# Modulation sums and convolution taps as multiply-add chains in PSUM; first three panels k-block by k-block

## The reference, cut to what matters

```python
def adaln(c, w_mod, b_mod):
    mod = jax.nn.silu(c) @ w_mod + b_mod
    return jnp.split(mod, 6, axis=-1)

def modulate(x, g, shift, scale):
    return rmsnorm(x, g) * (1.0 + scale[:, None, :]) + shift[:, None, :]
```

## Time and profile before

| | us |
|---|---|
| median of 3 runs | 2796.45 |
| the profiled execution | 2796.17 |
| its span | 2794.4 |
| PE busy | 2526.6 (90%) |
| DVE busy | 1561.7 (56%) |
| POOL busy | 954.9 (34%) |
| ACT busy | 908.9 (33%) |

### The profile page before, as it was taken

One profiled execution on the slowest core, in us unless ns is written; L12 is line 12 of the kernel. 1 busy time (PEld: TensorE's weight loads), 2 busy tenths in 40 slices (PEclk: granted clock), 3 DMA queues, 4 the chain that ended last, 5 costly groups with the idle time before them and its releaser, 6 DMA issues.

```text
span 2794.4 us, 35608 instructions
## 1 busy us (share of the span) xinstructions
PE 2526.6 (90%) x12106; PEld 2075.1 (74%) x12106; DVE 1561.7 (56%) x2371; ACT 908.9 (33%) x1433; POOL 954.9 (34%) x399
## 2 busy tenths in 40 slices
PE   5687998999998989899999834999999999999998
PEld 4567776787886667788887733888887887888886
DVE  6994567686634785311115995555455745463545
ACT  2150443322233253322224222332225544342222
POOL 1230003444453301344444531444444420344443
PEclk9895799999999899999999966999999999999999
DMA  6532003555432101232322200232223310232322
GB/s 265 173 128 83 1 17 131 178 185 176 147 106 76 61 9 68 75 98 90 99 97 91 83 30 17 96 105 90 98 90 105 98 61 1 83 105 91 98 95 70
DMA packets 71623, 263.70 MB, mean 94 GB/s; under 512 B 7904, under 2 KB 8416, under 8 KB 70880
## 3 DMA queue, kind: packets, MB, share of 16 engines
q1 hardware_dynamic: 68352, 251.01, 27.1%
q10 hardware_dynamic: 3168, 11.34, 1.1%
HBM read 260.22 MB, written 2.10 MB: 94 GB/s over the span
## 4 chain that ended last, share of the span: by engine, by line
PE 71%; issue 14%; DVE 10%; DVEq 2%; POOL 2%; ACT 1%; DMA 0%; POOLq 0%; ACTq 0%; SPq 0%
PE bank L562 21%; PE bank L563 21%; PE bank L564 21%; DVE cout L1808 3%; PE bank L707 2%; POOL w_lo L533 2%; PE bank L695 1%; PE bank L685 1%; DVE acc L1240 1%; DVEq L1801 1%; PE bank L849 1%; DVE tn L1292 1%; DVE h_lo L1287 1%; PE bank L641 1%; DVE modsum L1513 1%
## 5 line engine op out<-in xcount | busy, mean ns | idle before, releaser
L533 POOL TENSOR_TENSOR w_lo<-raw,w_hi 128x1024 fp32r<-128x1024 f32 x378 | 927.7, 2460 | 1811.8 <-ACT w_hi L921 1811.0
L562 PE MATMUL bank<-h_hi,w_hi 128*128 128x512 f32 x1760 | 708.7, 403 | 44.4 <-DVE h_lo L1287 19.5
L563 PE MATMUL bank<-h_lo,w_hi 128*128 128x512 f32 x1760 | 696.1, 396 | 0.0
L564 PE MATMUL bank<-h_hi,w_lo 128*128 128x512 f32 x1760 | 694.7, 395 | 0.0
L921 ACT ACTIVATE w_hi<-raw 128x1024 fp32r<-128x1024 f32 x378 | 393.5, 1052 | 594.9 <-PE bank L564 565.3
L562 PEld LDWEIGHTS bank<-h_hi,w_hi 128*128 128x128 f32 x1760 | 336.7, 191 | 133.6 <-issue 28.4
L562 PE MATMUL bank<-g_hi,w_hi 128*128 128x512 f32 x1072 | 421.5, 393 | 7.2 <-DVE g_lo L1391 5.6
L563 PE MATMUL bank<-g_lo,w_hi 128*128 128x512 f32 x1072 | 419.0, 391 | 0.0
L564 PE MATMUL bank<-g_hi,w_lo 128*128 128x512 f32 x1072 | 418.6, 390 | 0.0
L564 PEld LDWEIGHTS bank<-h_hi,w_lo 128*128 128x128 f32 x1760 | 336.6, 191 | 72.0
L563 PEld LDWEIGHTS bank<-h_lo,w_hi 128*128 128x128 f32 x1760 | 337.1, 192 | 67.6 <-issue 1.2
(11 more groups left out here) (260 smaller groups left out, 2807.6 us busy)
## 6 DMA issues: line engine op xcount, KB each, us to landing
raw<-in_panels SPq DMA_DIRECT2D x378, 512.0 KB, 3.7
modraw<-in_mods SPq DMA_DIRECT2D x80, 512.0 KB, 3.8
first_mods<-in_mods SPq DMA_DIRECT2D x4, 2048.0 KB, 19.8
w<-in_w ACTq DMA_DIRECT2D x2, 2048.0 KB, 8.6
x<-in_x SPq DMA_DIRECT2D x1, 2048.0 KB, 8.2
out<-yout ACTq DMA_DIRECT2D x8, 256.0 KB, 2.2
mask<-in_causal ACTq DMA_DIRECT2D x1, 1024.0 KB, 4.7
mask<-in_dilated ACTq DMA_DIRECT2D x1, 1024.0 KB, 4.8
```

The costliest lines, as they stand in the source:

```text
L533: pool.tensor_tensor(w_lo[:, slot, :], raw[:, slot, :], w_hi[:, slot, :].bitcast(F32), ALU.subtract)\
L562: pe.matmul(out, w_h, m_h, start=start, stop=False)
L563: pe.matmul(out, w_h, m_l, start=False, stop=False)
L564: return pe.matmul(out, w_l, m_h, start=False, stop=stop)
```

## The change

Five things. The sum of a modulation panel over k-blocks becomes a chain of eight instructions, one tensor_scalar and seven scalar_tensor_tensor, whose partial sum stands in PSUM (`CHAIN`, bank 6), with a drain between any two; it takes two panels at once (128x256 elements), which come in one load of 1 MB into one buffer, and PE sums both. The pairs go beside the odd panels up to 73, and beside P_OUT0 + 2, + 4 and + 6. The first 16 columns become four batches, each with two blocks of shift and two of scale; in a batch DVE sums three and PE does one, and the h of two k-blocks follows each batch. The sum of squares of the first norm is added up by PE over eight separate tiles (`sq0`). The first three panels behind the norms of layer 0, of layer 0's FFN, of layer 1 and of layer 1's FFN run k-block by k-block: nine matmuls per block, in three banks (`by_k`). The taps of the first three chunks of the 31-tap convolution are summed in banks 7, 4 and 6, and the last tap writes `cout`; the mixing matmuls move to banks 0 and 1.

```diff
+PAIR_AT = {}
+for _p in range(MOD_UNTIL):
+    if _p % 2 or _p in (P_OUT0 + 2, P_OUT0 + 4, P_OUT0 + 6):
+        PAIR_AT[_p] = len(PAIR_AT)
...
+            def load_pair(m, after):
+                sp_.wait_ge(mod_summed, after)
+                sp_.dma_start(modraw[:, :, :], A["pairs"][m]).then_inc(mod_landed, 16)
...
+            load_first(0)
+            for p in range(3):
                 load_raw(p)
...
+            for n in range(1, BATCHES):
+                load_first(n)
+            load_raw(3)
...
+            for p in range(P_FFN0):
                 load_raw(p + RING, after=p + 1)
...
+                if PAIR_AT.get(p, 0) > 0:
+                    load_pair(PAIR_AT[p], summed(PAIR_AT[p] - 1))
...
+            def first_batch(n):
+                pe.wait_ge(first_landed[n], 16)
+                if n == 3:
+                    pe.wait_ge(first_added, 1)
                 for k in range(KB):
-                    m = pe.matmul(mod_column(q), first_mods[q // 4][:, q % 4, P * k:P * k + P], csil[:, k:k + 1],
-                                  start=(k == 0), stop=(k == KB - 1))
+                    pe.matmul(FIRST_BANK[n][:, 0:1], first_mods[n][:, 0, P * k:P * k + P], csil[:, k:k + 1],
+                              start=(k == 0), stop=(k == KB - 1))
+                pe.wait_ge(mod_summed, n + 1)
+                for w in range(1, 4):
+                    m = pe.matmul(FIRST_BANK[n][:, w:w + 1], modsum[:, w, :], ones[:, 0:1], start=True, stop=True)
                 m.then_inc(mod_used, 1)
-            def mod_panel(slot, summed, out):
-                pe.wait_ge(mod_summed, summed)
-                pe.matmul(out, modsum[:, slot, :], ones[:, 0:1], start=True, stop=True).then_inc(mod_used, 1)
+            def mod_pair(m, summed_value, column):
+                pe.wait_ge(mod_summed, summed_value)
+                for w in range(2):
+                    last = pe.matmul(column(w), modsum[:, 2 * (m % 2) + w, :], ones[:, 0:1], start=True, stop=True)
+                last.then_inc(mod_used, 1)
...
+            def by_k(p, m_hi, m_lo, ready, ks):
+                for k in ks:
+                    pe.wait_ge(h_lo_ready, ready + k + 1)
+                    for slot in range(p % RING, p % RING + 3):
+                        if k == 0:
+                            pe.wait_ge(lo_ready, p + slot - p % RING + 1)
+                            if p >= RING:
+                                pe.wait_ge(bank_free, p + slot - p % RING - RING + 1)
+                        at = slot % RING
+                        wh, wl = w_hi[:, at, P * k:P * k + P], w_lo[:, at, P * k:P * k + P]
+                        m = three(bank[at][:, :], wh, wl, m_hi[:, k, :], m_lo[:, k, :], k == 0, k == KB - 1)
+                        if k == KB - 1:
+                            m.then_inc(panel_done, 1)
...
+                    elif n == 0:
+                        by_k(p, *up, KB * H_OF[r], range(KB))
+                        panel(p + 3, (p + 3) % RING, *up)
+                        for q in range(p, p + 4):
+                            with_mods(q)
+                        begun = 4
+                    panels(p + begun, 2 * size - begun, *up, mods=p < MOD_UNTIL)
...
-            rstd(0)
-            for q in range(MOD_FIRST):
-                if q in ALONE:
-                    first_mod_alone(q)
-                else:
-                    mod_panel(summed(q) % SUMS, summed(q), mod_column(q))
+            for k in range(KB):
+                pe.wait_ge(squares_ready, k + 1)
+                for j in range(QB):
+                    m = pe.matmul(bank[j][:, 0:1], sq0[:, k, P * j:P * j + P], ones[:, 0:1], start=(k == 0), stop=(k == KB - 1))
+            m.then_inc(sums_ready, 1)
+            first_batch(0)
+            spread(0, bank[5], QB)
+            first_batch(1)
+            by_k(0, h_hi, h_lo, 0, (0, 1))
+            first_batch(2)
+            by_k(0, h_hi, h_lo, 0, (2, 3))
+            first_batch(3)
+            by_k(0, h_hi, h_lo, 0, (4, 5, 6, 7))
...
             for n in range(KB):
-                square(0, n, x[:, n, :])
-            take_root(0)
...
+                act.activation(sq0[:, n, :], x[:, n, :], ACT.Square).then_inc(squares_ready, 1)
+            for p in range(3):
+                split_hi(p)
+            act.wait_ge(sums_ready, 1)
+            for j in range(QB):
+                m = act.activation(root[:, j:j + 1], bank[j][:, 0:1], ACT.Sqrt, bias=EPS, scale=1.0 / D)
+            m.then_inc(root_ready, 1)
+            act.dma_start(lruw[:, :, :, :], A["lruw"]).then_inc(lru_landed, 16)
...
-                                sum_mod_loop(it, pg + AHEAD)
-                                sum_mod_loop(it, pu + AHEAD)
+                                m = PAIR_AT[pu + AHEAD]
+                                sum_pair(m, it * 32 + 16 * (m + 1), it * 2 + (summed(m) - 2))
                         dve.drain()
...
+            def weighted(blocks_, n, to, used):
+                w = blocks_.rearrange("p n (k m) -> p n k m", m=P)
+                part = CHAIN[:, 0:n * P].rearrange("p (n m) -> p n m", m=P)
+                dve.tensor_scalar(part, w[:, :, 0, :], csil[:, 0:1], None, MUL)
+                for k in range(1, KB):
+                    dve.drain()
+                    if k == KB - 1 and used is not None:
+                        dve.wait_ge(mod_used, used)
+                    m = dve.scalar_tensor_tensor(out=part if k < KB - 1 else to, in0=w[:, :, k, :], scalar=csil[:, k:k + 1],
+                                                 in1=part, op0=MUL, op1=ADD)
+                m.then_inc(mod_summed, 1)
+                dve.drain()
+            def sum_first(n):
+                dve.wait_ge(first_landed[n], 16)
+                weighted(first_mods[n][:, 1:4, :], 3, modsum[:, 1:4, :], n if n else None)
+            def sum_pair(m, landed, used):
+                dve.wait_ge(mod_landed, landed)
+                at = 2 * (m % 2)
+                weighted(modraw[:, :, :], 2, modsum[:, at:at + 2, :], used)
...
+            def by_part(v_, n):
+                return v_.rearrange("p (w k) -> p w k", w=2)[:, :, 2 * n:2 * n + 2]
+            def first_h(n):
+                dve.wait_ge(mod_used, n + 1)
+                dve.tensor_tensor(by_part(modv[:, 0:2 * KB], n), FIRST_BANK[n][:, 0:4].rearrange("p (w k) -> p w k", w=2),
+                                  by_part(cols[:, COLS["modb"]:COLS["modb"] + 2 * KB], n), ADD).then_inc(first_added, 1)
+                dve.drain()
+                at = COLS["g0mix"] + 2 * n
+                dve.scalar_tensor_tensor(out=gains[:, 2 * n:2 * n + 2], in0=modv[:, KB + 2 * n:KB + 2 * n + 2], scalar=1.0,
+                                         in1=cols[:, at:at + 2], op0=ADD, op1=MUL)
+                if n == 0:
+                    dve.wait_ge(rstd_ready, 1)
+                dve.drain()
+                for k in (2 * n, 2 * n + 1):
+                    dve.scalar_tensor_tensor(out=tn[:, k % 2, :], in0=x[:, k, :], scalar=gain(0, k), in1=bank[5][:, :],
+                                             op0=MUL, op1=MUL).then_inc(t_ready, 1)
+                dve.drain()
+                for k in (2 * n, 2 * n + 1):
+                    dve.wait_ge(h_hi_ready, k + 1)
+                    dve.scalar_tensor_tensor(out=h_lo[:, k, :], in0=tn[:, k % 2, :], scalar=shift(0, k),
+                                             in1=h_hi[:, k, :].bitcast(F32), op0=ADD, op1=SUB).then_inc(h_lo_ready, 1)
+                dve.drain()
+            dve.wait_ge(csil_ready, 1)
+            sum_first(0)
+            invert_root(0)
+            sum_first(1)
+            first_h(0)
+            sum_first(2)
+            first_h(1)
+            sum_first(3)
+            first_h(2)
+            first_h(3)
+            dve.memset(axp[:, :, 0:TAPS_LRU - 1], 0.0)
...
+                    part = bank[TAP_BANK[c]][:, :] if c < 3 else cout[:, c, :]
                     if k == 0:
-                        dve.tensor_scalar(cout[:, c, :], pad[:, c, 0:T], col("cconv", c), col("cconvb", c), MUL, ADD)
+                        dve.tensor_scalar(part, pad[:, c, 0:T], col("cconv", c), col("cconvb", c), MUL, ADD)
                     else:
-                        dve.scalar_tensor_tensor(out=cout[:, c, :], in0=pad[:, c, k:k + T], scalar=col("cconv", 4 * k + c),
-                                                 in1=cout[:, c, :], op0=MUL, op1=ADD)
+                        dve.scalar_tensor_tensor(out=cout[:, c, :] if k == TAPS_CONV - 1 else part, in0=pad[:, c, k:k + T],
+                                                 scalar=col("cconv", 4 * k + c), in1=part, op0=MUL, op1=ADD)
             for c in range(4):
```

More of the change, by code:

```diff
@@ L362, in build @@
         DVE_TAPS3 = taps_beside(P_OUT2)[0]
+        TAP_BANK = (7, 4, 6)
         block = ctx.enter_context(nc.Block())
@@ L377, in build @@
         LAST_BY_PE = (1, 2, 3, 10)
-        ADD_AT = [SQ_AT[r] - sum(q < r for q in LAST_BY_PE) for r in range(12)]
```

(24 more changed lines are left out.)

131 lines of the change are left out of this document (50 added, 81 removed).

## The result

| | before | after |
|---|---|---|
| median, us (runs) | 2796.49 (4) | 2712.26 (4) |
| lowest to highest | 2793.66 to 2799.84 | 2704.73 to 2716.94 |
| the profiled execution, its span | 2796.17, 2794.4 | 2709.95, 2708.2 |

What follows compares the result with a forecast made beforehand. PE bounds the kernel, with gains only where it waits beside a full DVE. Start -52, projection +15, k-by-k panels -10 and convolution -30 sum to -77: 2719 us from 2796.45, range 2695 to 2755.

Steps and rivals of the forecast that it cites:

- What bounds: Whole kernel: PE busy 2526.6 of 2794.4 us; gains only where PE waits and DVE is nearly full.
- A step of the chain: Modulation sums in PSUM: a pair's eight steps cost 4.5 us (4.2 to 5.5), a first batch 5.5.
- A tap in PSUM: Convolution taps: 0.75 us each with the accumulator in PSUM, against a mean of 1.145 before.
- Start: Start to the hidden layer's first matmul: from 224 to 172 us, -52 (bounds -43 and -60).
- Projection: Layer 0's output projection: seven pairs in a row behind one load buffer, 10.1 us a cycle, +15 (+10 to +30).
- By k: First three panels behind the norms: 18.4 us instead of 22.4, 2 left in layer 0's FFN, -10 in all.
- Convolution: Layer 2's convolution: DVE's taps stop stretching, ACT and POOL bound next, statistics start at 1622, -30 (-24 to -37).
- 1: Modulation chain no cheaper than multiply and reduce, about 6.5 us a pair: 2756 us in all; chance 0.15.
- 2: Convolution: POOL takes DVE's place as bound, only 15 of 30 us come: 2734 us in all; chance 0.13.
- 3: Pair's load becomes the bound wherever modulation runs; at 9 us landing the kernel is slower, 2830 us; chance 0.04.
- 4: More than forecast: PE's clock high from the first k-by-k block, POOL's rounds shorter: 2699 us; chance 0.10.

Runs made afterwards that it cites:

- three panels of lead: Kernel before, with DVE's modulation sums in layer 0's FFN three panels ahead of PE instead of two: 2796.17 us, ratio 0.9995.
- the ten taps: Changed kernel with ten DVE taps moved forward to its idle places, ten fourth-chunk taps from the tail to the mixing outputs: 2700.9 us, ratio 0.9647.
- late loads: Changed kernel with ACT's loads of w1, the masks and w_small issued at about 88 us instead of 55: 2708.81 us, ratio 0.9691.

## Why the prediction was right, point by point

- **What bounds** was read rightly: the gain lies where DVE was full. It missed one thing. "PE is busy for 258 of 260, and nothing done on DVE is worth anything there" fails in layer 0's FFN, which gained 7.0 us where I had 2. PE's ends are modelled, so a wait of 0.25 us for modsum at every second panel counts as busy. The starts of successive matmuls show it, and three panels of lead gave back 5.3 us. With the 2 us of by_k that makes the 7.
- **A step of the chain**: 0.56 us from start to start, 4.4 us a pair (4.5 taken), 5.5 a first batch (5.5). A tap in PSUM 0.752 (0.75), none above 0.758.
- **Start**: -48.7 for -52, with errors that cancel, so the closeness is partly luck. "The last h ends at about 63" was wrong by 7 us: it ends at 55.6, since DVE, not PE, sets the pace of the last two batches (low parts at 50.64 and 54.19). Then "9 x 4.5 instead of 84.9" left out the loads, 16.3 us of waiting in four pairs. I had priced the single buffer for the projection and forgot it where the same pairs follow each other at the start. The forecast's own sum with the measured terms is 55.6 + 147 - 84.9 + 40.1 + 16.3 = 174, against 175.4 measured, so the 6 us that it added for PE's panels, gates and scans were not needed. Panels 0 to 2 end at 61.5 and not at 69.
- **Projection**: +11.1 for +15. Seven sums in a row, DVE waiting for the load six times, 16.1 us in all; the cycle is 9.4 us (the sums end from 356.5 to 412.8, in six steps), not 10.1, and the last add_x comes 62 us after the first matmul, not 67. With three pairs in the place of seven the whole loss is gone. The 4 us too many in the forecast are six cycles of 4.45 + 0.1 + 4.85 us, where 4.5 + 0.4 + 5.2 were taken.
- **By k**: -4 and -4 as forecast; at layer 0's FFN 2, by the run without it. PE meets the pair of the fourth panel as said:

```profile
447.07 0.50 PE L590 MATMUL bank<-ones,modsum 128*128 128x1 f32 x4
449.53 0.61 PE L590 MATMUL bank<-ones,modsum 128*128 128x1 f32 x4 [1.96 <-DVE modsum L1560]
```

- **Convolution**: -31.2 for -30. PE's part was read rightly: its second v pair ends 77.4 us behind the copy of rb, for 77. That DVE no longer bounds is shown by the ten taps that cost nothing in front of the statistics. The mixing matmuls start 100.8 us behind the copy of rb (102 forecast, 132 before). POOL's eight rounds are where luck helped: they were to run back to back at 6.1 us and set the end. Each takes 5.3 instead, since the adds take 1.29 us where they took 1.62 (which I had as a bound only), and POOL then stands idle for 7.1 us, waiting for ACT's rounding, which waits for PE. So PE and then ACT's own work of 12.7 us set the time, and POOL only 2.2 us of it. The rule of the Trainium skill ("GPSIMD Engine Reference", section "Key points") that GpSimd shares its SBUF interfaces with DVE's instructions of two SBUF inputs agrees with the three runs on it here (the taps in PSUM, POOL's adds left out, the chain in SBUF). The one in "VectorE: DVE Perf Modes", section "The TRN2 errata — SBUF-src ops pay a fixed extra latency per instruction", which would add an estimated 65 ns to a step with a PSUM source, does not: 489 ns with the sum in PSUM, 485 in SBUF.
- **The rivals**: 1 is out by the chain's 4.4 us. 2 is out: POOL's rounds got shorter. 3 has the right form, but its landing of 9 us was far off: even two megabytes land in about 7. 4 is half there (POOL), and was not needed.
- The last 2.8 us lie in stretches with the same instructions, and they are PE's clock: at layer 2's output projection seven matmuls run at the slow pitch of 0.43 us where thirteen did before, and in layer 3's first panel (at 2019.5 us, before at 2104.3) none does where eight did. That is 14 x 0.2 us. The version with the taps alone has the same 1071.8 us there; the forecast had nothing for it.

## What to carry to other kernels

When a VectorE instruction with two SBUF inputs has a mean well above its median, look whether GpSimd runs beside it, and put its accumulator in PSUM: this alone was worth 31 us in a stage of 190, and both engines gain. It takes a free PSUM bank. Before work is spread over a pipeline with a single load buffer, write down its cycle (sum, gap, landing) for every stretch where it recurs, and put it where the consuming engine is idle by the windows: placing the same 40 pairs elsewhere was worth a further 29 us. A PE that is 99% busy by its modelled ends can still wait; compare the starts.

## What the runs showed of the hardware, unexpected

- POOL and a VectorE instruction with two SBUF inputs do not share time, they take turns. In each of the four shapes looked at, every instruction of this kind that began while POOL worked ended a fixed time behind POOL's end: 0.55 us for 512 elements per partition (29 of 29 taps), 1.08 for 1024 (36 of 36 modulation multiplies, L1508 in the kernel before, 30 us lost in all), and with the chain in SBUF 0.28 for 256 (27 of 27) and 0.41 for 384 (4 of 4). That is about 1.07 ns per element each time, as if none of its work had been done before POOL ended. The reductions with one SBUF input (L1513) never grew, though 44 of 80 overlapped with POOL.
- The granted clock in the same stretch can differ between executions of nearly one program. In the windows behind the hidden layer's first half, the changed kernel (columns as in the windows above):

```profile
190.00:215.00 25.00, 23.96 (x163) 23.83 (x162) 1.67 (x4) 3.21 (x4) 4.66 (x2) 0.77 0.45 168
```

  With late loads:

```profile
187.00:212.00 25.00, 23.96 (x197) 23.84 (x196) 1.67 (x4) 4.71 (x6) 4.67 (x2) 0.93 0.45 169
```

  In the same 25 us PE does 197 matmuls instead of 163, and the stretch to the projection takes 167.3 us instead of 176.7. Eight other versions, the kernel before among them, show 0.77 there, with 162 or 163 matmuls. Whether the later loads raised the clock or chance did is not shown; the profiled execution was the fastest of its four by 9 us, which speaks for chance. Such differences are why a stage is compared by landmarks here, not by the whole time.
- The first step of a chain, a tensor_scalar, is the one that pays for writing PSUM: 0.81 us against 0.55 for a tap, 0.486 against 0.368 at the median for a pair (0.348 at the least). The seven steps behind it do not. The Trainium skill ("VectorE: DVE Perf Modes", section "The perf-mode tier table") has a doubled rate for this operation in fp32 with SBUF operands and, under "Why PSUM operands drop a tier", the single rate in fp32 with any operand in PSUM. The runs here look like that: at 1.07 ns per element (above), 512 elements take an estimated 0.27 us less at the doubled rate, and the difference is 0.265. With its sum in SBUF the first step, too, was held up by POOL: 15 of 40 times, each ending 0.15 us behind POOL, about half of the 0.28 of a step behind it.
